# Cutting GpSimd subtractions into shorter instructions in a two-layer hybrid attention kernel

## What is computed

```python
def mixer_block(h, ...):                      # h: [1, 528, 1024]
    proj = rms_norm(h, norm1_g) @ w_in        # 1024 -> 5544 columns
    fq, fk, fv, ff, cq, ckv, krope, sq, sk, sv, gates = split(proj)
    out_a = causal_attention(rms(fq), rms(fk), fv, cumsum(log_sigmoid(ff + b)))   # 8 heads of 64
    out_b = causal_attention(q(cq), k(ckv, krope), v(ckv))                        # 8 heads of 96, latent
    out_c = sliding_window_attention(rms(sq), rms(sk), sv, sinks, slopes)         # 8 heads of 64, 2 kv heads
    y = einsum('blnc,ncd->blnd', [out_a, out_b, out_c], w_branch)
    return h + sum(sigmoid(gates) * y, axis=2) @ w_o

def conv_ffn(h, ...):
    u = rms_norm(h, norm2_g) @ w_up           # 1024 -> 5632
    gate, val = split(conv_b + causal_conv3(u, conv_w))
    return h + (silu(gate) * val) @ w_down    # 2816 -> 1024
```

## Time and profile before

| | us |
|---|---|
| median of three runs | 1999.71 (1999.29 to 2000.68) |
| the profiled execution's own time | 1999.88 |
| its span, from the first to the last instruction | 1998.1 |

### The profile page before, as it was taken

One profiled execution on the slowest core, in us unless ns is written; L12 is line 12 of the kernel. 1 busy time (PEld: TensorE's weight loads), 2 busy tenths in 40 slices (PEclk: granted clock), 3 DMA queues, 4 the chain that ended last, 5 costly groups with the idle time before them and its releaser, 6 DMA issues.

```text
span 1998.1 us, 36507 instructions
## 1 busy us (share of the span) xinstructions
PE 1925.1 (96%) x14436; PEld 1825.6 (91%) x14436; DVE 1158.6 (58%) x2125; ACT 762.9 (38%) x1463; POOL 1024.3 (51%) x1306
## 2 busy tenths in 40 slices
PE   6899999998999999999998999999999999999999
PEld 6889998888999999999997899988889999999887
DVE  7665476787464666652246654767865656566411
ACT  4555566555223222220035556666552232222100
POOL 7656554554354544455476565544534545545553
PEclk9999999999999999999999999999999999999999
DMA  4212111111132332223332121112112323332332
GB/s 148 73 45 65 54 60 48 54 54 53 56 127 85 96 96 85 86 94 96 95 107 75 43 65 55 62 45 64 44 53 64 129 86 95 96 96 87 104 95 95
DMA packets 44803, 156.32 MB, mean 78 GB/s; under 512 B 5012, under 2 KB 5268, under 8 KB 44504
## 3 DMA queue, kind: packets, MB, share of 16 engines
q1 hardware_dynamic: 44488, 153.75, 24.5%
q10 hardware_dynamic: 144, 0.22, 0.0%
HBM read 149.63 MB, written 4.26 MB: 77 GB/s over the span
## 4 chain that ended last, share of the span: by engine, by line
PE 78%; DVE 12%; ACT 4%; issue 3%; POOL 2%; DMA 0%; ACTq 0%; DVEq 0%; POOLq 0%
PE ps L1336 20%; PE ps L1339 20%; PE ps L1341 19%; PE ps L1567 5%; PE ps L1351 2%; PE ps L1347 2%; PE ps L1350 2%; PE ps L1355 2%; DVE rstd L1670 2%; PE ps L1480 1%; PE ps L1519 1%; DVE osum L1978 1%; DVE ps L1947 1%; PE ps L1525 1%; POOL wl L809 1%
## 5 line engine op out<-in xcount | busy, mean ns | idle before, releaser
L809 POOL TENSOR_TENSOR wl<-raw,wh 128x256 fp32r<-128x256 f32 x1076 | 793.6, 769 | 751.6 <-DVE wh L1649 743.8
L1336 PE MATMUL ps<-xh,wh 128*128 128x264 f32 (+1 forms) x2880 | 811.2, 303 | 21.7 <-DVE wl L1729 10.2
L1339 PE MATMUL ps<-xl,wh 128*128 128x264 f32 (+1 forms) x2880 | 764.0, 285 | 0.0
L1336 PEld LDWEIGHTS ps<-xh,wh 128*128 128x128 f32 x2880 | 546.9, 190 | 42.0 <-issue 27.0
L1341 PE MATMUL ps<-xh,wl 128*128 128x264 f32 (+1 forms) x2880 | 584.3, 284 | 0.0
L1339 PEld LDWEIGHTS ps<-xl,wh 128*128 128x128 f32 x2880 | 546.8, 190 | 17.1 <-issue 9.2
L1341 PEld LDWEIGHTS ps<-xh,wl 128*128 128x128 f32 x2880 | 450.8, 190 | 0.0
L1649 DVE CAST wh<-raw 128x1024 fp32r<-128x1024 f32 x270 | 201.9, 748 | 174.4 <-PE ps L1336 91.5
L1970 DVE TENSOR_TENSOR ps<-ps,cst 128x128 f32<-128x128 f32 (+6 forms) x240 | 75.1, 315 | 153.7 <-PE ps L1525 112.2
L1567 PE MATMUL ps<-pt,vx 128*128 128x512 f32 (+7 forms) x480 | 158.4, 411 | 2.7 <-ACT pt L1253 2.5
L1253 ACT ACTIVATE pt<-ps 128x256 f32<-128x256 f32 (+5 forms) x224 | 77.8, 363 | 102.5 <-DVE ps L1970 101.5
(11 more groups left out here) (194 smaller groups left out, 3413.6 us busy)
## 6 DMA issues: line engine op xcount, KB each, us to landing
raw<-weights SPq DMA_DIRECT2D x270, 512.0 KB, 3.5
h<-tokens SPq DMA_DIRECT2D x4, 528.0 KB, 6.7
h<-tokens SPq DMA_DIRECT2D x8, 264.0 KB, 4.8
residual<-h SPq DMA_DIRECT2D x8, 264.0 KB, 4.8
h<-residual SPq DMA_DIRECT2D x8, 264.0 KB, 5.2
out<-h SPq DMA_DIRECT2D x8, 256.0 KB, 4.6
cst<-constants SPq DMA_DIRECT2D x1, 1048.0 KB
extra<-positions SPq DMA_DIRECT2D x18, 4.1 KB
```

Of the source, the lines that this page charges most:

```text
L809: ins = nc.gpsimd.tensor_tensor(wl[c % SPLIT][:, part], raw[:, c % RAW, part], wh[c % SPLIT][:, part].bitcast(F32), ALU.subtract)
L1336: a = nc.tensor.matmul(out, a_hi, x_hi[:, sl], start=first, stop=False)
L1339: nc.tensor.matmul(out, a_hi, x_lo[:, sl], start=False, stop=False)
```

## The change

`chunk_low` issues eight subtractions of 128 x 128 for a chunk instead of four of 128 x 256. The subtractions of queries, keys, latents and heads go through a new function `less`, which issues four of 132 columns instead of one of 528. The values that are computed are the same. As before, only the last piece of a subtraction ticks the semaphore, there are no waits between pieces, and nothing else moves: no buffer, no order of steps and no other engine's instruction is changed.

```diff
+LOW_PARTS = 4
+LOW_PIECE = P
@@ chunk_low
-                for a in range(0, CW, CW // 4):
-                    part = slice(a, a + CW // 4)
+                for a in range(0, CW, LOW_PIECE):
+                    part = slice(a, a + LOW_PIECE)
                     ins = nc.gpsimd.tensor_tensor(wl[c % SPLIT][:, part], raw[:, c % RAW, part],
                                                   wh[c % SPLIT][:, part].bitcast(F32), ALU.subtract)
                 ins.then_inc(s_lo, 1)
@@ new
+            def less(dst, whole, high):
+                for a in range(0, T, T // LOW_PARTS):
+                    part = slice(a, a + T // LOW_PARTS)
+                    ins = nc.gpsimd.tensor_tensor(dst[:, part], whole[:, part], high[:, part], ALU.subtract)
+                return ins
@@ one of the eight places that now call it
-                                nc.gpsimd.tensor_tensor(yq[own, i, e, :], q32[own, t.n % 2, :],
-                                                        xq[own, i, e, :].bitcast(F32), ALU.subtract).then_inc(
+                                less(yq[own, i, e, :], q32[own, t.n % 2, :], xq[own, i, e, :].bitcast(F32)).then_inc(
                                     query_low.sem, query_low.tick((l, j, e)))
```

More of the change, by code:

```diff
@@ L943, in _ @@
                                 settled()
-                                nc.gpsimd.tensor_tensor(yk[other, i, e, 1:T + 1], q32[own, t.n % 2, :],
-                                                        xk[own, i, e, 1:T + 1].bitcast(F32), ALU.subtract).then_inc(
+                                less(yk[other, i, e, 1:T + 1], q32[own, t.n % 2, :], xk[own, i, e, 1:T + 1].bitcast(F32)).then_inc(
                                     key_low.sem, key_low.tick((l, j, e)))
@@ L950, in _ @@
                             settled()
-                            nc.gpsimd.tensor_tensor(skl[:, :], q32[:, t.n % 2, :], skh[:, :].bitcast(F32),
-                                                    ALU.subtract).then_inc(key_low.sem, key_low.tick((l, "sk")))
+                            less(skl[:, :], q32[:, t.n % 2, :], skh[:, :].bitcast(F32)).then_inc(key_low.sem, key_low.tick((l, "sk")))
                             began["last"] = (key_low.sem, key_low.n)
@@ L957, in _ @@
                                 settled()
-                                nc.gpsimd.tensor_tensor(latl[:, k, :], q32[:, k, :], lath[:, k, :].bitcast(F32),
-                                                        ALU.subtract).then_inc(
+                                less(latl[:, k, :], q32[:, k, :], lath[:, k, :].bitcast(F32)).then_inc(
                                     latent_ready.sem, latent_ready.tick((l, k)))
@@ L964, in _ @@
                             settled()
-                            nc.gpsimd.tensor_tensor(latl[:, 2, :], q32[:, 0, :], lath[:, 2, :].bitcast(F32),
-                                                    ALU.subtract).then_inc(
+                            less(latl[:, 2, :], q32[:, 0, :], lath[:, 2, :].bitcast(F32)).then_inc(
                                 latent_ready.sem, latent_ready.tick((l, 2)))
@@ L972, in _ @@
                             settled()
-                            nc.gpsimd.tensor_tensor(yq[0:MQ, j % 2, e, :], q32[0:MQ, t.n % 2, :],
-                                                    xq[0:MQ, j % 2, e, :].bitcast(F32), ALU.subtract).then_inc(
+                            less(yq[0:MQ, j % 2, e, :], q32[0:MQ, t.n % 2, :], xq[0:MQ, j % 2, e, :].bitcast(F32)).then_inc(
                                 query_low.sem, query_low.tick((l, j, e)))
@@ L981, in _ @@
                                 settled()
-                                nc.gpsimd.tensor_tensor(yk[0:MQ, j % 2, e, 1:T + 1], q32[0:MQ, e, :],
-                                                        xk[0:MQ, j % 2, e, 1:T + 1].bitcast(F32),
-                                                        ALU.subtract).then_inc(
+                                less(yk[0:MQ, j % 2, e, 1:T + 1], q32[0:MQ, e, :], xk[0:MQ, j % 2, e, 1:T + 1].bitcast(F32)).then_inc(
                                     key_low.sem, key_low.tick((l, j, e)))
@@ L990, in _ @@
                         settled()
-                        nc.gpsimd.tensor_tensor(otl[:, ot_at(j), :], oraw[:, :], oth[:, ot_at(j), :].bitcast(F32),
-                                                ALU.subtract).then_inc(heads_low.sem, heads_low.tick((l, j)))
+                        less(otl[:, ot_at(j), :], oraw[:, :], oth[:, ot_at(j), :].bitcast(F32)).then_inc(heads_low.sem, heads_low.tick((l, j)))
                         began["last"] = (heads_low.sem, heads_low.n)
```

## The result

The changed kernel takes **2028.9 us** (median of 4 runs, 2026.5 to 2029.2) beside 1999.6 for the kernel before on the same chip: ratio **1.0145 [1.0133, 1.0157]**, 29 us slower. The forecast was 1992, its range ended at 2005. The profiled execution has a span of 2026.9.

A forecast was written before the change was run, and what follows sets the result against it. PE was taken as the bound, busy 1925 of 1998 us. 12.0 us won from shorter waits and less slow clock, minus 4.2 lost at layer and feed-forward starts, gave 7.8 less: 1992 us, 8-in-10 range 1983 to 2005.

The forecast's parts named there:

- The wait behind a short piece: DVE instructions stopped by a POOL subtraction: 0.16 us at 128 columns, 0.17 at 132, instead of 0.44 and 1.03.
- The first rival: DVE's wait behind a piece falls only to 0.28 us; 2.8 us won, 1997 us; chance 0.24.
- The mid-kernel waits: PE waits on DVE chains at 115, 304, 366, 475, 1113, 1303, 1363 and 1471 us shorten by 6.5 together, four fifths taken.
- slow stretches: Half-clock PE time behind shortened waits at 304, 475 or 1471, 1113 and 1304 goes: 8.5 us, four fifths taken.
- POOL's own time: Eight pieces take 3.4 us, 0.57 more a chunk, about 150 us busy; activations some 45 us; mostly covered by idling.
- The layer starts: DVE's gain is undone by POOL's late chunk near 60 and 1060 us: 0.9 us lost in layer 0, 2.2 in layer 1.
- the first chunks: At the kernel's start: come out even, more turns for the second chunk, fewer fills disturbed by DVE afterwards.
- The feed-forward starts: PE begins a chunk at once when ready, so POOL's 0.57 us goes straight to PE in both layers: 1.1 lost.
- the second rival: POOL becomes the late engine at layer starts and chunks queued behind `yq` or `yk`; 6 us lost, 2006; chance 0.17.

The follow-up runs named there:

- the padded kernel: Kernel before, plus a POOL fill of 400 columns ahead of each weight chunk and 220 ahead of each 528-column subtraction, no cuts: 2015.79 us, 1.0087.

## Why the prediction was wrong, point by point

- **The wait behind a short piece: right.** 0.17 forecast, 0.14 measured; `rstd`'s longest 0.86 against "near 0.9". The first rival (0.28) is out. The prediction held that the rule of the Trainium skill (SBUF — State Buffer, SBUF: two separate sides), a lock for the whole instruction, leads to it; but that rule names no share of the duration, and the rows nearly agree with it. `otl` takes 1.63 us where 1.33 are usual, so it got going 0.30 after 297.70, 0.13 before `square` ended (298.13); and the 0.71 of `rstd` ran from 299.19 to its end at 299.90, so from 0.14 before `otl` ended (299.33). These two overlaps, and 0.03 between two DVE instructions, are the 0.3 us by which a stop is shorter than POOL's instruction.
- **The mid-kernel waits: right in size.** nm, ptm and the waits for xk (at 366 and 1363) together fell by 5.8 us; 6.5 with a discount of a fifth is 5.2. Three slow stretches that I had named (at 475, 1113 and 1471) are gone. How much of that the short pieces did is not shown: in the trace of the kernel before with early rows nm and ptm wait the same 9.3 and 3.6 us, and the granted clock is 1.00 at 1113 and 1471 all the same.
- **POOL's own time: right for a piece, short in the sum.** Eight pieces without DVE take 3.3 to 3.4 us, forecast 3.4. In all POOL is busy 1312, forecast 1220. The 92 us between are turns with DVE: I priced these in one burst at the layer start and let the 150 us for the chunks stand as if no DVE instruction passed elsewhere. wl alone rose by 218, where 150 were forecast: 218 of its pieces took over 0.52 us, and before only 80 of the 256-column ones over 0.78.
- **The layer starts: the wait right, what follows it too small.** In layer 1 the gain of the DVE chain (3.9 forecast, 3.8 measured), PE's wait (6.3 and 6.13) and its resuming (2.4 late, measured 18.15 - 15.6 = 2.5) came as worked out. Behind that I put 1.7 for the clock and took 1.9 off for the next waits, which PE's lateness should absorb. But the clock stays low for 6.0 us after the wait, which costs 3.0, and of the next waits only nmx shrank (1.26 to 0.56); sq is 1.45 where it was 1.47. With 1.6 lost ahead of it (a matmul at 1029.87 comes 14.0 late, that at 1037.93 15.6, since PE's wait for wl between them grew from 1.09 to 2.69; I had the chunk at 1032.53 end "1.5 later" and took that to shift the chain at no cost), the start costs 20.4 - 14.0 = 6.4 against 2.2. In layer 0 I had counted 1.7 us more room and a loss of 0.9. PE waited 6.22 all the same, and its lateness grows from the 1.8 of the first chunks, which I had called even, to 6.1: 4.3 against 0.9.
- **The feed-forward starts: short.** PE waits 0.70 in layer 0, and 0.25 and 0.74 in layer 1, 1.7 in all against 1.1, and its lateness grows by 2.1. Ahead of them in layer 1 comes a wait for DVE (`h`, 0.95 us at 1624.39) that the kernel before did not have, for another 1.1.
- **The missed step: the extra key rows.** This is most of the size of the loss; with the rows early the kernel is still 6 us slower than before, for which the layer starts and the first chunks are enough. I asked where PE *waits* for POOL and where a *chunk* has room, and never asked what else POOL hands to PE. The casts stand in POOL's queue behind `otl`, `yk` and a chunk, all of which the change makes longer, by 2.3 us together in the three lines shown. At the first place they were 0.3 us ahead of PE, no more than the hand-over takes; at the other five 1.35 to 3.38 us, which the lateness gathered in POOL's queue used up. My ground for pricing the middle of the layers at nothing, "POOL idles 744 us" and a chunk "usually ready 3 us or more ahead of PE", spoke of chunks only. Early rows give back 24 of the 29 us. The mechanism is that of the second rival ("any chunk queued behind a `yq` or `yk`"), but it looked at chunks alone and at 6 us of loss.
- **The sum.** Forecast 7.8 won, measured 28.8 lost between the two profiled executions, 36.6 apart. By PE's lateness: rows 27.6 against nothing; first chunks 1.8 against nothing; the start of layer 0 4.3 against 0.9, that of layer 1 6.4 against 2.2; feed-forward starts 2.1 against 1.1; the wait for `h` 1.1 against nothing. That is 43.3 lost, so 14.5 were won elsewhere, against 12.0: 4.4 at 304, 3.0 at 1303, some 2 each at 475, 1113 and 1471. The gains did not fail, though part of them may be luck: the trace of the kernel before with early rows ends 4.1 us ahead too, 1.2 to 1.6 of it each at 305, 1113, 1303 and 1471, with the waits for nm and ptm unchanged.

**What stays open.** How much of the loss is POOL's own added time and how much are turns with DVE: the padded kernel was to tell it, but its fills also push the subtractions into more of DVE's casts. No run adds time to POOL while its subtractions meet DVE as before. Nor does a run separate the clock's part of the gains from chance, with one trace of each kernel.

## What to carry to other kernels

Before you make an engine's work longer or finer, list everything that it hands over, also what nobody waits for now, with the time between ready and used: a hand-over without a wait may have no room at all, and a late engine can reach the bottleneck through the queue of a third. Cut long instructions only where the engine that pays has room, and move its small urgent items ahead of the large ones first; here that, with the chunks left at four pieces, turned 1.0145 into 0.9955. Two parts that each cost a little may cost twice their sum, because both use up the same room.

## What the runs showed of the hardware

- DVE's stop behind one POOL piece is always some 0.3 us less than POOL's instruction takes, so it falls faster than the duration: 1.03 us at 528 columns, 0.44 at 256, and 0.14 at 128, behind instructions of 1.33, 0.74 and 0.46 us.
- Between two pieces a DVE instruction can pass, so cutting multiplies POOL's turns: eight pieces of 128 take 3.4 us alone and 6.35 beside a dense DVE.
- What a wait costs in clock differs: in the changed kernel nothing behind one of 2.69 (at 1052) and one of 1.92 (at 1263), 1.5 us behind one of 2.88 (3.3 us at half the clock, at 133), 2.1 behind one of 6.22 (4.2 us, at 67) and 3.0 behind one of 6.13 (6.0 us, at 1079).
- A POOL fill of 400 columns takes 0.435 us, 1.1 ns a column where a subtraction of 256 columns takes 2.9 (0.74 us). A fill and DVE's `rstd`, which stops for subtractions, run side by side at their usual length.
- A hand-over from POOL to a waiting PE took 0.3 us from the end of the last cast (132.83) to PE's start (133.12).
